# Attention scores of two heads side by side in a table of small tasks, with mask steps moved by at most a slab

## The reference, cut to what matters

```python
s = jnp.einsum("bnqkgd,bnskd->bnkgqs", qb, kb) * (HEAD_DIM ** -0.5)
s = jnp.where(mask[None, :, None, None, :, :], s, NEG_INF)
m = jnp.maximum(jnp.max(s, axis=-1, keepdims=True), sink)
p = jnp.exp(s - m)
denom = jnp.sum(p, axis=-1, keepdims=True) + jnp.exp(sink - m)
o = jnp.einsum("bnkgqs,bnskd->bnqkgd", p / denom, vb)
```

## Time and profile before

| what | value |
|---|---|
| median of 3 runs | 2149.07 us |
| span of the profiled execution | 2148.6 us |
| PE busy | 2126.1 us, 99% |
| DVE busy | 1640.3 us, 76% |
| ACT busy | 1212.5 us, 56% |
| DMA | 376.54 MB, mean 175 GB/s |
| heads of scores before, first layer (slab that they follow) | 0 (31); 1, 2 (33); 3, 4 (35); 5 (36); 6, 7 (38) |
| heads of scores before, second layer | 0, 1 (27); 2 (29); 3, 4 (33); 5, 6 (36); 7 (37) |

### The profile page before, as it was taken

How to read it: one execution, slowest core, us unless ns; L and a number is a source line. 1 busy time by engine, 2 the same in 40 slices (tenths; PEclk the granted TensorE clock), 3 DMA queues, 4 the chain that set the end, 5 groups by cost and what they waited for, 6 DMA issues and landing times.

```text
span 2148.6 us, 47945 instructions
## 1 busy us (share of the span) xinstructions
PE 2126.1 (99%) x18740; PEld 2069.0 (96%) x18740; DVE 1640.3 (76%) x2626; ACT 1212.5 (56%) x1823; POOL 56.4 (3%) x54
## 2 busy tenths in 40 slices
PE   9999999999999999999999999999999999999998
PEld 8999999999999999899999999999899999999998
DVE  8997877987778766778947877766678947877764
ACT  6646544556656445446658845445446658845443
POOL 0000000000000000000002200000000002200000
PEclk9999999999999999999999999999999999999999
DMA  7434655644456556554544466556554544465553
GB/s 250 158 129 149 207 187 185 201 160 150 138 167 216 185 195 208 171 169 145 177 157 152 149 199 207 187 188 214 172 167 147 177 157 150 149 200 186 187 189 128
DMA packets 102977, 376.54 MB, mean 175 GB/s; under 512 B 11681, under 2 KB 11809, under 8 KB 102305
## 3 DMA queue, kind: packets, MB, share of 16 engines
q1 hardware_dynamic: 101664, 368.66, 52.1%
q10 hardware_dynamic: 1152, 5.58, 0.7%
HBM read 373.14 MB, written 1.05 MB: 174 GB/s over the span
## 4 chain that ended last, share of the span: by engine, by line
PE 90%; DVE 6%; ACT 2%; issue 1%; DMA 0%; DVEq 0%; ACTq 0%
PE acc L772 25%; PE acc L774 24%; PE acc L773 24%; DVE w_lo L1806 2%; PE acc L891 1%; PE acc L892 1%; PE acc L893 1%; PE acc L837 1%; PE acc L836 1%; PE acc L838 1%; ACT w_hi L1325 1%; PE mid L1128 1%; PE mid L1227 1%; DVE pr L2565 0%; PE mid L959 0%
## 5 line engine op out<-in xcount | busy, mean ns | idle before, releaser
L1806 DVE TENSOR_TENSOR w_lo<-w_raw,w_hi 128x1024 fp32r<-128x1024 f32 x694 | 848.0, 1226 | 317.0 <-ACT w_hi L1325 308.7
L1325 ACT CAST w_hi<-w_raw 128x1024 fp32r<-128x1024 f32 x694 | 724.1, 1047 | 537.9 <-PE acc L774 473.1
L772 PE MATMUL acc<-h_hi,w_hi 128*128 128x256 f32 x2096 | 597.2, 285 | 0.3 <-DVE w_lo L1806 0.3
L774 PE MATMUL acc<-h_hi,w_lo 128*128 128x256 f32 x2096 | 586.0, 280 | 0.0
L773 PE MATMUL acc<-h_lo,w_hi 128*128 128x256 f32 x2096 | 585.0, 279 | 0.4 <-issue 0.4
L772 PE MATMUL acc<-g_hi,w_hi 128*128 128x256 f32 x1456 | 409.3, 281 | 0.8 <-DVE w_lo L1806 0.7
L774 PE MATMUL acc<-g_hi,w_lo 128*128 128x256 f32 x1456 | 406.6, 279 | 0.0
L773 PE MATMUL acc<-g_lo,w_hi 128*128 128x256 f32 x1456 | 406.1, 279 | 0.0
L772 PEld LDWEIGHTS acc<-h_hi,w_hi 128*128 128x128 f32 x2096 | 394.7, 188 | 6.6 <-issue 4.9
L773 PEld LDWEIGHTS acc<-h_lo,w_hi 128*128 128x128 f32 x2096 | 394.1, 188 | 1.1 <-issue 0.6
L774 PEld LDWEIGHTS acc<-h_hi,w_lo 128*128 128x128 f32 x2096 | 394.5, 188 | 0.0
(11 more groups left out here) (443 smaller groups left out, 3455.6 us busy)
## 6 DMA issues: line engine op xcount, KB each, us to landing
w_raw<-weights_d SPq DMA_DIRECT2D x695, 512.0 KB, 3.5
p<-p_d ACTq DMA_DIRECT2D x3, 1080.0 KB, 8.5
rdec<-decay_d ACTq DMA_DIRECT2D x2, 768.0 KB, 5.1
p<-p_d SPq DMA_DIRECT2D x1, 1024.0 KB, 10.5
out_d<-work SPq DMA_DIRECT2D x4, 256.0 KB, 2.3
x_all<-x_d SPq DMA_DIRECT2D x1, 516.0 KB, 4.3
w_raw<-weights_d SPq DMA_DIRECT2D x2, 256.0 KB, 5.7
x_all<-x_d SPq DMA_DIRECT2D x1, 512.0 KB, 6.1
```

The costliest lines, as they stand in the source:

```text
L772: mm(dst, wh, hi[:, k, :], start=first and j == 0, stop=False)
L774: done = mm(dst, wl, hi[:, k, :], start=False, stop=last and j == len(ks) - 1)
L1325: nc.scalar.copy(w_hi[:, slot, :], w_raw[:, slot, :]).then_inc(hi_done, 1)
L1806: tt(w_lo[:, slot, :], w_raw[:, slot, :], w_hi[:, slot, :].bitcast(F32), SUB).then_inc(lo_v, 1)
```

## The change

In the two tables of `ORDER1` the tasks `scores` and `mask` are put elsewhere; nothing is added or taken away, and no wait, bank or buffer differs. Both layers now have the scores of heads 0 and 1, 2 and 3, 4 and 5, 6 and 7 next to each other, behind the slabs 31, 34, 36, 38 in the first layer and 27, 32, 34, 36 in the second. Two of the lines, first layer above and second below:

```diff
-        36: (("mask", 4), ("turn",), ("scores", 5)),
+        36: (("turn",), ("scores", 4), ("scores", 5)),
+        37: (("mask", 4),),
...
-        29: (("scores", 2), ("turn",)),
-        32: (("mask", 0), ("mask", 1), ("mask", 2)),
+        29: (("turn",),),
+        32: (("mask", 0), ("mask", 1), ("scores", 2), ("scores", 3)),
```

More of the change, by code:

```diff
@@ L151 @@
         30: (("rot", 2), ("rot", 3)),
[L152 to L155, removed]
-        36: (("mask", 4), ("turn",), ("scores", 5)),
-        38: (("scores", 6), ("scores", 7), ("mask", 5)),
+        31: (("scores", 0), ("scores", 1), ("mask", 0), ("scan",)),
+        34: (("mask", 1), ("scores", 2), ("scores", 3)),
+        35: (("mask", 2), ("mask", 3)),
+        36: (("turn",), ("scores", 4), ("scores", 5)),
+        37: (("mask", 4),),
+        38: (("mask", 5), ("scores", 6), ("scores", 7)),
         39: (("mask", 6), ("mask", 7)),
@@ L191 @@
         27: (("scores", 0), ("scores", 1)),
-        29: (("scores", 2), ("turn",)),
-        32: (("mask", 0), ("mask", 1), ("mask", 2)),
[L194 to L197, removed]
+        29: (("turn",),),
+        32: (("mask", 0), ("mask", 1), ("scores", 2), ("scores", 3)),
+        33: (("mask", 2), ("mask", 3)),
+        34: (("out_power", 1), ("scores", 4), ("scores", 5)),
+        35: (("mask", 4),),
+        36: (("out_power", 2), ("mask", 5), ("scores", 6), ("scores", 7)),
+        37: (("out_power", 3), ("mask", 6), ("mask", 7), ("maxima",)),
         40: (("cx",), ("softmax",), ("normalize",)),
```

## The result

The changed kernel takes 2155.22 us, median of 6 runs (2154.72 to 2156.10). The kernel before takes 2148.24 us beside it, median of 6 runs (2147.45 to 2149.98). The ratio is 1.0031, 95% interval 1.0021 to 1.0041, so the change costs 4.5 to 8.8 us where 3.8 were forecast. Two later sets of runs on other chips, 7 and 11 of the change, gave 5.7 and 5.3 us more than before in the mean. The range of the prediction ended at 2154.5 us.

The account below looks back on a forecast made before the run. PE, busy 99% of the span, was taken to bound the kernel. Layer losses of 1.65 and 2.16 us, net of pairing's gain, sum to 3.81 us on 2149.07: 2152.9 us, chance 0.70, range 2151.4 to 2154.5 us.

Parts of the forecast that it names:

- What bounds the kernel, and the price of a visit: PE bounds; a scores visit costs 1.05 us (one head) or 1.07 (two), so pairing saves 1.03 us per layer.
- The first layer's wait: PE at head 7's scores waits for head 4's mask behind the turn, 1.8 us real pause; slab 39 starts 1.65 us later.
- starts at 135.00, as before: First layer, DVE: split of slab 39 keeps its start, having waited for ACT's rounded copy, which the change doesn't touch.
- The second layer's wait: PE at head 3's scores waits for head 0's mask, about 2.2 us real pause; slab 34 2.14 later, layer loses 2.16 us.
- the sum: Both layers' losses, 1.65 + 2.16 = 3.81 us, on the profiled span of 2148.6 us: 2152.4 us.
- The other waits, and what could be given back: Other masks come in time for PE; nothing counted back, bounds zero and 1.1 us of waits for ACT's copies.
- absorbed: Rival: PE finds up to 1.1 us of its waits for ACT's copies already paid, 2151.8 us; chance 0.06.
- The base: Time before the change: median of the runs 0.5 us above the profiled span, 2149.07 us.
- The clock: Rival: granted clock falls behind the new pauses, 1.6 us a fall; 2154.5 us once, 2156.1 twice; chance 0.12.
- whether the pause of the second layer is enough: Condition for the clock rival: 2.2 us pause lies between a 2.5 us one with a fall and 2.0 without.
- The issue pauses: Rivals: PE's 0.9 us pause in the state-space output vanishes (2152.0 us, chance 0.04) or another appears (2153.8 us, 0.05).

Follow-up runs that it names:

- second and third traces of the change: Changed kernel, unaltered, profiled again beside the kernel before: medians 2156.07 us (7 runs, +5.7 us) and 2154.76 us (11 runs, +5.3 us).
- second trace of the kernel before: Kernel before, unchanged, profiled in another execution; stretches holding the moved tasks 42.24 us (first layer) and 41.91 us (second).
- pairs with early masks: Changed kernel with masks of head 4 (first layer) and head 0 (second layer) moved ahead of the turn: median 2149.16 us, 0.9998 of before.
- early masks in the second layer: Kernel before with pairs and an early mask of head 0 in the second layer only: median 2149.03 us, 0.9992 of before.

## Why the prediction was wrong

**What bounds the kernel, and the price of a visit**: right. Where no wait stands in the way, pairing is worth 1.05 us in the second layer's stretch, 1.03 forecast.

**The first layer's wait**: right in place and cause, too large in size. Head 7 was to wait 1.8 us by itself and slab 39 to start 1.65 us later; the traces have pauses of 1.28 to 1.34 us, and ACT's evacuations on the two sides stand 6.12 us apart in the first, where 6.5 was read. Slab 39 starts 1.60 us later there, but 0.31 us of that is another wait, at the first visit, for rotated states of DVE: PE came to slab 31 1.3 us earlier than in the rows, and DVE's part of that stage didn't move with it. The kernel before has the same wait in its second trace, whose stretch is 42.24 us. Like beside like, the change's stretch is 43.47 us for 42.24 with this wait, and 43.03 and 43.01 for 41.86 without: 1.15 to 1.23 us lost. The forecast's term is some 0.45 us too large, because the split of slab 39 "starts at 135.00, as before" was not a fixed time. It waited for ACT's copy, and in that one execution the copy had itself waited for the slab's load:

```profile
133.92 1.05 ACT L1325 CAST w_hi<-w_raw 128x1024 fp32r<-128x1024 f32 x1 [0.39 <-DMA w_raw<-weights_d]
```

In the second and third traces of the change the load is there in time, and the split, the turn and the mask of head 4 all stand 0.47 us earlier against slab 31 than the forecast has them, while PE reaches heads 6 and 7 where it was forecast.

**The second layer's wait**: right. 2.14 us of pause for 2.2, slab 34 2.1 us later for 2.14, the stretch 2.0 us longer. Both layers' stretches together lose 3.2 us, where the sum has 3.81.

**The other waits, and what could be given back**: right. No other wait for a mask is in the list, and nothing of the shift was absorbed; the waits for ACT's copies stay at 1.1 us.

**The base** was sound within a microsecond: the kernel before took 2149.5 to 2150.0 us in the median of the three later sets, for 2149.1, and the 2148.2 beside the result is some 1.5 us lower, which goes with its difference of 7.0 us where the later sets have 5.3 and 5.7.

**The clock is the step that failed.** The sum put it at nothing, and in the mean over the runs it has some 2 us. It stood among the rivals, with the right mechanism and the right price for one fall (1.6 us; 1.5 measured, in three traces). Its chance of 0.12 was wrong, and so was the form of the question, "whether the pause of the second layer is enough". I set two stretches of one trace beside each other, one with a fall behind a pause of 2.5 us and one without behind 2.0 us, and took a limit to lie between them, with the first of the new pauses below it and the second in doubt. Other executions cut that line down. In the second trace of the kernel before, the pause of 2.4 us behind which the clock had fallen:

```profile
102.10:105.50 3.40, 0.96 (x76) 0.80 (x68) 3.01 (x5) 1.15 (x2) 0.00 (x0) 1.00 0.05 17
105.50:109.00 3.50, 3.50 (x55) 3.28 (x57) 2.29 (x3) 3.39 (x7) 0.00 (x0) 1.00 0.02 5
```

Here it stays at 1.00. And in the trace of pairs with early masks, the pause of 2.0 us behind which it had stayed:

```profile
497.40:500.80 3.40, 1.61 (x41) 1.57 (x41) 2.98 (x6) 3.28 (x9) 0.00 (x0) 1.00 0.65 182
500.80:504.20 3.40, 3.40 (x17) 3.19 (x16) 2.57 (x2) 1.82 (x3) 0.00 (x0) 0.50 0.36 134
```

Here it falls. And in the trace of the changed kernel, around the first of these places again, with a pause of 1.9 us:

```profile
102.10:105.50 3.40, 1.54 (x81) 1.28 (x71) 3.01 (x5) 1.25 (x3) 0.00 (x0) 1.00 0.02 5
105.50:109.00 3.50, 3.50 (x19) 3.50 (x18) 2.24 (x4) 3.26 (x5) 0.00 (x0) 0.51 0.02 5
```

PE did more here than where it stayed at 1.00. So there is no such line: a pause of either length brings a fall in some executions. Of the 14 traces, 9 have a fall at this place, behind issue pauses of 1.8 to 2.5 us, and 5 have none, behind 1.6 to 2.4 us; near 500 us it is 3, behind 1.9 to 2.0 us, and 11, behind 1.4 to 2.0. Behind the first layer's 1.3 us it came in 2 of 5 traces, behind the second layer's 2.15 us in 2 of 4, behind 3.3 us in the only one, and never where the wait was filled, shortened or absent. The Trainium skill, page "TensorE: Matmul & The Clock Gate", section "HAM oscillation — how this bites in real kernels", looks for this in longer idle gaps than these, at waits for data that come back every turn of a loop; the falls behind 1.3 and 2.15 us here differ from that, and the measurement decides.

What it costs in all: sorted by the granted clock, the spans tell the two parts of the loss apart. At 0.998 the kernel before takes 2147.6 us (53 runs) and the change 2151.5 (3 of its 18); at 0.997 it is 2149.2 (9 runs) and 2152.7 (7). That is 4.0 and 3.5 us more at the same clock, near the 3.81 of the sum and the 3.2 of the stretches; with so few runs, spread by 1.4 us, it can't choose between them. But the change is at 0.997 or 0.996 in 14 of these 18 runs, the kernel before at 0.998 or 0.999 in 73 of 82. The rest of the 5.3 to 5.7 us is that shift. By mean clocks, 0.9969 for 0.9980 to 0.9983, it would be 2.4 to 3.0 us; by the difference of the times it is 1.5 to 1.9 beyond the sum, 2.1 to 2.5 beyond the stretches. It can't be told more closely. One run's mean clock is a poor witness of a fall: in every trace the last 4.7 to 7.6 us of the span are at 0.50, behind PE's last matmul, and this end alone moves the mean by up to 0.0007, as much as a fall of 3.4 us (0.0008). So 0.9982 and 0.9989 both belong to traces without a fall (the kernel before again, early masks in the second layer). Over 11 and 27 runs that evens out.

With hindsight, 3.8 us for the waits and half a fall for each of them, 1.6 us, would have said 2154.5 us, for the measured 2155.2; the half is read from these traces and wasn't known before.

**The issue pauses** vary by up to 0.7 us from execution to execution of one program (PE's waits of this kind sum to 6.63 and 5.91 us in the two traces of before, 6.70, 7.43 and 6.71 us in the three of the change), so neither rival of them can be called true or false.

## What to carry to other kernels

Before two tasks are paired on an engine, look at what the other engine has queued ahead of the one that frees the second task's buffer: here a turn of 7 us stood in front of a mask of 0.8 us, and a saving of 1.0 us per layer became a loss of 1.2 to 2.1. A pause that you give the matrix engine costs its own length and a chance of some microseconds at half clock behind it; put it in the sum as a share of a fall, not as a case of its own, and move the releasing work forward, or, failing that, fill the pause (worth about 1.5 us here, the waits' own 3.2 stay). One profiled execution shows one outcome of that chance, so read the mean granted clock of all runs beside it. And before a row's start is taken over as fixed, follow what it waited for back to the end: here a load that was late in that one execution put 0.45 us into the sum.

## What the runs showed of the hardware

- The granted clock fell to 0.50 behind pauses of PE of 1.3 us in some executions and stayed at 1.00 behind 2.4 us in others, with PE busy before and behind in both.
- A fall lasted 3.4 or 6.8 us in the records. A short one cost 1.5 us in each of three traces. The long one followed a pause of 1.3 us once and cost 3.1 us, and one of 3.3 us once, where it began 0.8 us ahead of the pause's end and cost 2.7.
- The mean granted clock of a run counts half-clock time that costs nothing: in all 14 traces the clock is at 0.50 for the last 4.7 to 7.6 us of the span, behind PE's last matmul.
- PE pauses of 0.5 to 2.5 us that nothing in the profile ends stand in stages of many small matmuls, at much the same places, and change in length by up to 0.7 us between executions of the same program; some of them stand in one execution and not in another.
